# Rotation, key decay and key masks of a retention/GLA mixer on GpSimd instead of VectorE, and its constants loaded in three groups

## The reference, cut to what matters

```python
proj = rmsnorm(x, w_norm_mix) @ w_in
q_r, k_r, v_r, g_r, q_g, k_g, v_g, g_g, a_lr = split(proj)
q_r = rotary(q_r, pos)
k_r = rotary(k_r, pos) * DK ** -0.5
# retention, per chunk
scores = (q_r @ k_r.T) * decay_mask
out    = scores @ v + (q_r @ S) * q_decay
S      = S * chunk_decay + (k_r * k_decay).T @ v
# gated linear attention (GLA): the same form, with data-dependent decays exp(cumsum(log_a))
x = x + concat(norm(out_r) * silu(g_r), norm(out_g) * silu(g_g)) @ w_out
# then: rmsnorm -> PEER expert retrieval (16384 experts) -> residual -> final rmsnorm
```

## Time and profile before

| | |
|---|---|
| median of 3 runs | 4079.37 us (4070.77 to 4085.7) |
| profiled execution, its own time | 4075.24 us |
| its span, first to last instruction | 4073.5 us |
| mixer, from SyncE's first load to the first load of the next stage | 677.90 to 969.90 us, 292 us |
| TensorE matmul busy | 3608.8 us (89%) |
| VectorE busy | 2568.2 us (63%) |
| GpSimd busy | 1355.0 us (33%) |
| mean granted TensorE clock | 0.932 |

### The profile page before, as it was taken

One profiled execution on the slowest core, in us unless ns is written; L12 is line 12 of the kernel. 1 busy time (PEld: TensorE's weight loads), 2 busy tenths in 40 slices (PEclk: granted clock), 3 DMA queues, 4 the chain that ended last, 5 costly groups with the idle time before them and its releaser, 6 DMA issues. The chain is left out here.

```text
span 4073.5 us, 49975 instructions
## 1 busy us (share of the span) xinstructions
PE 3608.8 (89%) x19469; PEld 3360.9 (83%) x19469; DVE 2568.2 (63%) x3509; ACT 1083.2 (27%) x984; POOL 1355.0 (33%) x990
## 2 busy tenths in 40 slices
PE   6999996885986969987998998999599999999996
PEld 5888885664865859987998998998599999999995
DVE  4111112885213118999777777777688888898886
ACT  3222221332112213322333333332122222222222
POOL 0000000000000000111978888886154455454442
PEclk8999998776997989998999999999799999999997
DMA  4222223435323544554888989888788898989886
GB/s 161 108 108 108 108 98 109 145 120 187 132 79 140 196 156 146 218 214 172 334 332 332 345 318 354 334 318 349 289 332 334 336 353 339 357 332 357 343 328 230
DMA packets 209787, 983.08 MB, mean 241 GB/s; under 512 B 20593, under 2 KB 84401, under 8 KB 111202
## 3 DMA queue, kind: packets, MB, share of 16 engines
q1 hardware_dynamic: 130898, 523.57, 34.5%
q0 software_dynamic: 60960, 424.18, 27.2%
q10 hardware_dynamic: 17776, 33.27, 2.3%
HBM read 873.43 MB, written 107.52 MB: 241 GB/s over the span
## 5 line engine op out<-in xcount | busy, mean ns | idle before, releaser
L2062 PE MATMUL outputs_vp<-outputs_w_hi,outputs_whi 128*128 128x384 f32 x2048 | 693.0, 338 | 78.2 <-DVE outputs_w_lo L1994 41.3
L1624 PE MATMUL hidden_hp<-hidden_dense_hi,hidden_whi 128*128 128x384 f32 x2048 | 710.1, 347 | 42.0 <-DVE hidden_wlo L1408 41.9
L1625 PE MATMUL hidden_hp<-hidden_dense_lo,hidden_whi 128*128 128x384 f32 x2048 | 697.4, 341 | 0.0
L1626 PE MATMUL hidden_hp<-hidden_dense_hi,hidden_wlo 128*128 128x384 f32 x2048 | 696.5, 340 | 0.0
L2064 PE MATMUL outputs_vp<-outputs_w_hi,outputs_wlo 128*128 128x384 f32 x2048 | 691.1, 337 | 0.0
L2063 PE MATMUL outputs_vp<-outputs_w_lo,outputs_whi 128*128 128x384 f32 x2048 | 691.0, 337 | 0.0
L1553 POOL DMA_INDIRECT hidden_row<-u_rows,expert_ids x192 | 334.2, 1740 | 952.1 <-DVEq L1806 713.1
L1827 DVE CUSTOM_DVE_ANT_0 hidden_row<-hidden_row,hidden_h_row 128x2048 f32<-128x2048 f32 x192 | 439.4, 2298 | 175.2 <-DMA hidden_row<-u_rows,expert_ids 174.0
L1877 POOL DMA_INDIRECT outputs_row<-v_rows,outputs_id x192 | 321.1, 1672 | 618.9 <-DVE accg L2011 575.5
L1566 POOL TENSOR_SCALAR hidden_spare<-hidden_iota,hidden_seconds 128x128 f32<-128x128 f32 x384 | 476.1, 1252 | 122.9 <-PE hidden_tq L1609 78.2
L1404 ACT CAST outputs_whi<-outputs_raw 128x2048 fp32r<-128x2048 f32 x128 | 244.9, 1913 | 851.0 <-PE outputs_vp L2064 601.1
(11 more groups left out here) (313 smaller groups left out, 5041.4 us busy)
## 6 DMA issues: line engine op xcount, KB each, us to landing
hidden_raw<-u_units SPq DMA_DIRECT2D x128, 1024.0 KB, 8.0
outputs_raw<-v_units SPq DMA_DIRECT2D x128, 1024.0 KB, 6.5
w_in_raw<-w_in SPq DMA_DIRECT2D x48, 1024.0 KB, 5.2
hidden<-hidden_hid SPq DMA_DIRECT2D x128, 192.0 KB, 3.7
gate_mat<-hidden_big SPq DMA_DIRECT2D x12, 2048.0 KB, 14.2
outputs_w<-hidden SPq DMA_DIRECT2D x16, 1536.0 KB, 13.0
outputs_g<-gate_mat SPq DMA_DIRECT2D x16, 1536.0 KB, 21.9
w_out_raw<-w_out SPq DMA_DIRECT2D x16, 1024.0 KB, 5.7
```

Source lines behind the costliest of these rows:

```text
L1624: mm(o, un.hi[s][:, x, :], h_hi[:, x, :], start=x == 0, stop=False)
L1625: mm(o, un.hi[s][:, x, :], h_lo[:, x, :], start=False, stop=False)
L1626: ins = mm(o, un.lo[s][:, x, :], h_hi[:, x, :], start=False, stop=x == KT - 1)
L2062: mm(o, un.hi[x][:, at, :], W_hi[s][:, e, :], start=e == 0, stop=False)
```

## The change

In the mixer, `rotate` (with the decayed keys) and the making of `km` move from VectorE's program to GpSimd's, between its DMAs. `km` gets a function of its own, `mask_keys`. GpSimd's first two `move_in` come after `rotate(SMP)` and a wait for the first logarithm chain. The constants are in three groups with a semaphore each: nine for the sample tile (`const_s_in`), five for the prompt tiles (`const_in`), and `gnb` (`norm_in`). ScalarE no longer waits for constants. SyncE loads `alr` first, then `qk_r`, the nine, `qk_g`, the five, and then waits for the first rotation ahead of the samples' v and g.

```diff
+        consts_s = [(wa2, w_a2), (rope, c["rope"]), (kdec_s, c["kdec_s"]), (keep_s, c["keep_s"]), (ident, c["ident"]),
+                    (qdec_s, c["qdec_s"]), (mask_rs, c["mask_rs"]), (causal_s, c["causal_s"]), (seq_rows, c["seq_rows"])]
+        consts = [(keep, c["keep"]), (kdec, c["kdec"]), (qdec, c["qdec"]), (mask_r, c["mask_r"]), (causal, c["causal"])]
...
+            sp.wait_ge(ones_set, 1)
+            sp.dma_start(alr[0:RANK, :], alr_dram).then_inc(alr_in, 16)
             load_qk_r(SMP)
+            for tile_, src in consts_s:
+                sp.dma_start(tile_[:], src).then_inc(const_s_in, 16)
+            load_qk_g(SMP)
             for tile_, src in consts:
                 sp.dma_start(tile_[:], src).then_inc(const_in, 16)
-            sp.wait_ge(ones_set, 1)
-            sp.dma_start(alr[0:RANK, :], alr_dram).then_inc(alr_in, 16)
-            load_qk_g(SMP)
-            for n in range(3):
-                sp.dma_start(gnb[:, n, :], gn[n].partition_broadcast(P)).then_inc(const_in, 16)
+            load_qk_r(0)
             for g in range(2):
                 part(v_s[g], smp_in, SMP, (VR, VG)[g])
                 part(g_s[g], smp_in, SMP, (GR, GG)[g])
-            load_qk_r(0)
             load_vg_r(0)
             load_qk_g(0)
+            for n in range(3):
+                sp.dma_start(gnb[:, n, :], gn[n].partition_broadcast(P)).then_inc(norm_in, 16)
...
+            d = Steps(pool, pstep)
+            ptt, mult, sub = nc.gpsimd.tensor_tensor, ALU.mult, ALU.subtract
...
+            def mask_keys(k):
+                group, h = k // H, k % H
+                if group == 0:
+                    pool.wait_ge(k_decayed, 1)
+                else:
+                    pool.wait_ge(kl_copied, 1)
+                ks = (kd_s, klr_s)[group][:, h, :]
+                if k > 0:
+                    pool.wait_ge(st_made, st_at["head", k - 1, 1] + 1)
+                ptt(km[:], bcast(ks, 1, NSEQ), bcast(seq_rows[:], 2, DK), mult).then_inc(k_masked, 1)
+
+            pool.wait_ge(const_s_in, 16 * n_consts_s)
+            rotate(SMP)
+            pool.wait_ge(z_log, 1)
             move_in(0)
             move_in(1)
-            move_out(0)
-            store_r(0)
-            move_out(1)
-            for t in range(PTILES):
+            for t in [SMP] + list(range(PTILES)):
                 x, y = heads_at(t)
-                if t == 3:
+                if x is not None:
+                    if t == SMP:
+                        pool.wait_ge(const_in, 16 * n_consts)
+                    rotate((t + 1) % TILES)
+                if t != SMP:
+                    move_out(y - 2 if y else 2 * H - 1)
+                    store_r(t)
+                if x is None:
                     store_samples(1)
-                if t == 3:
                     store_g(t)
                     break
+                mask_keys(x)
                 move_out(x)
-                store_g(t)
+                if t != SMP:
+                    store_g(t)
                 if t == 1:
                     store_samples(0)
-                store_r(t + 1)
-                move_out(y)
+                mask_keys(y)
...
-            act.wait_ge(const_in, 16 * n_consts)
...
-            vec.wait_ge(const_in, 16 * n_consts)
+            vec.wait_ge(const_s_in, 16 * n_consts_s)
...
+                if t == 0:
+                    vec.wait_ge(norm_in, 48)
...
-                rotate(u)
                 mask_g_scores(t)
+                if smp:
+                    vec.wait_ge(const_in, 16 * n_consts)
...
-            pe.wait_ge(const_in, 16 * n_consts)
             pe.wait_ge(alr_in, 16)
+            pe.wait_ge(const_s_in, 16 * n_consts_s)
```

More of the change, by code:

```diff
@@ L605, in mixer @@
         s8_out = [a.gpsimd_dma_sem(f"s8_out{s}") for s in range(2)]
-        final_out, dstep, astep = a.sem("final_out"), a.sem("dstep"), a.sem("astep")
+        final_out, dstep, astep, pstep = (a.sem(s) for s in ("final_out", "dstep", "astep", "pstep"))
         block = ctx.enter_context(nc.Block())
@@ L649, in seg @@
             return at
-        n_consts = len(consts) + 3
+        n_consts_s, n_consts = len(consts_s), len(consts)
         @block.sync
@@ L737, in store_samples, with rotate @@
                                out_s[group][:].rearrange("p h v -> p (h v)")).then_inc(s_mix_stored, 16)
+            def rotate(t):
+                R, n = rows(t), front(t)
+                pool.wait_ge(qk_r_in, 16 * (n + 1))
+                cos, sin = (bcast(rope[0:R, t, x, :], 1, 8) for x in range(2))
+                x1, x2 = qk_r[0:R, :, 0:64], qk_r[0:R, :, 64:128]
+                wait(pool, r_turned, n)
+                wait(pool, k_decayed, n)
+                d(ptt(ra[0:R], x1, cos, mult))
+                d(ptt(rb[0:R], x2, sin, mult))
+                d.wait()
+                ptt(rot[0:R, :, 0:64], ra[0:R], rb[0:R], sub).then_inc(rotated, 1)
+                pool.wait_ge(rotated, 2 * n + 1)
+                d(ptt(ra[0:R], x1, sin, mult))
+                d(ptt(rb[0:R], x2, cos, mult))
+                d.wait()
+                ptt(rot[0:R, :, 64:128], ra[0:R], rb[0:R], ALU.add).then_inc(rotated, 1)
+                pool.wait_ge(rotated, 2 * n + 2)
+                if n > 1:
+                    pool.wait_ge(st_made, st_at["ret", t - 1] + 1)
+                k, by = (kd_s, kdec_s) if t == SMP else (kd, kdec)
+                ptt(k[0:R], rot[0:R, 4:8, :], bcast(by[:], 2, DK), mult).then_inc(k_decayed, 1)
@@ L879, in _ @@
             vec.wait_ge(zeros_set, 5)
-            vec.wait_ge(const_in, 16 * n_consts)
-            def rotate(t):
-                R, n = rows(t), front(t)
-                vec.wait_ge(qk_r_in, 16 * (n + 1))
-                cos, sin = (bcast(rope[0:R, t, x, :], 1, 8) for x in range(2))
-                x1, x2 = qk_r[0:R, :, 0:64], qk_r[0:R, :, 64:128]
-                wait(vec, r_turned, n)
-                wait(vec, k_decayed, n)
-                d(tt(ra[0:R], x1, cos, mult))
-                d(tt(rb[0:R], x2, sin, mult))
-                d.wait()
-                tt(rot[0:R, :, 0:64], ra[0:R], rb[0:R], sub).then_inc(rotated, 1)
-                vec.wait_ge(rotated, 2 * n + 1)
-                d(tt(ra[0:R], x1, sin, mult))
-                d(tt(rb[0:R], x2, cos, mult))
-                d.wait()
-                tt(rot[0:R, :, 64:128], ra[0:R], rb[0:R], ALU.add).then_inc(rotated, 1)
-                vec.wait_ge(rotated, 2 * n + 2)
-                if n > 1:
-                    vec.wait_ge(st_made, st_at["ret", t - 1] + 1)
-                k, by = (kd_s, kdec_s) if t == SMP else (kd, kdec)
-                tt(k[0:R], rot[0:R, 4:8, :], bcast(by[:], 2, DK), mult).then_inc(k_decayed, 1)
+            vec.wait_ge(const_s_in, 16 * n_consts_s)
             def decay_q(t):
@@ L1142, in finish_g @@
                     tt(o, o, g_g[:], mult).then_inc(g_mixed, 1)
-            rotate(SMP)
             log_decay(SMP)
```

16 lines of the change are left out of this document (3 added, 13 removed).

## The result

The changed kernel took **4089.9 us** (median of 14 runs, 4082.3 to 4095.8), the kernel before beside it 4079.6 us (14 runs): ratio **1.0023**, 95% interval 1.0013 to 1.0032. The forecast was 4075, 4.5 us faster; it became 10.3 us slower, 0.9 us above the range.

The account below looks back on a forecast made before the run. It took the mixer as bound by loads at its start, then by VectorE and TensorE handing work to and fro, VectorE waiting for scores. 8.5 - 2.5 - 1.5 = 4.5 us faster than 4079.37 gave 4075 us, range 4061 to 4089.

Parts of the forecast that it names:

- Part 5: VectorE and GpSimd meeting at SBUF, seven two-input finish_r operations held 0.27 us or less each: 1.5 us lost.
- Rival (b): VectorE held by GpSimd for whole operations in finish_r of three tiles: 2.8 us slower, 4082; chance 0.20.
- Part 3: Mixer start: gate 12 us earlier, less 1 for GpSimd's rotation and 2.5 for late g_r(0): 8.5 us gained.
- Part 1: Prompt tiles' rotation leaves VectorE, which then waits longer for TensorE's scores: 0 us.
- Part 2: Masked keys, eight operations of 1.21 us, leave VectorE and become longer waits for TensorE: 0 us.
- Part 4: Head 3's masked keys come late behind DMAs in GpSimd's queue, a new wait: 2.5 us lost.
- Rival (c): GpSimd's time follows element count, 2.43 and 4.86 us, delaying start and head 3's keys: 5.5 slower, 4085; chance 0.15.
- Rival (d): GpSimd's first operation starts late, or postponed transfers take back the gate's gain: 5 us less at start, 4080; chance 0.08.
- Rival (a): All of VectorE's relief counts: 24 us rotations, 9 key masks, 12 at the gate: 4034; chance 0.05.

Follow-up runs that it names:

- e1: The changed kernel with rotations and key masks back on VectorE, constant groups and load order kept: 4060.6 us, 0.9963 of the kernel before.
- e11: The kernel of e1 unchanged, measured once more: 4066.6 us, 0.9964 of the kernel before.
- e8: e1 plus four GpSimd memsets per pass into a buffer nobody reads: 4069.7 us, 0.9967 of the kernel before.
- e10: e1 with the samples' rotation alone on GpSimd: 4072.3 us, 0.9984 of the kernel before.
- e9: e1 with the rotations of tiles 1 to 3 on GpSimd, started only after weigh: 4068.1 us, 0.9968 of the kernel before.
- e2: The changed kernel with rotations back on VectorE and key masks still on GpSimd: 4068.4 us, 0.9985 of the kernel before.
- e4: The changed kernel with GpSimd's rotations of tiles 1 to 3 started only after weigh: 4073.2 us, 0.9996 of the kernel before.
- e12: e10 with g_r(0) loaded ahead of the samples' v and g: 4070.4 us, 0.9980 of the kernel before.

## Why the prediction was wrong

Against before, after's mixer has -8.8 at the start (`var_r(0)`), +23.7 held, -3.0 between score maskings and the next `var_r`, +0.5 at the end: +12.4. (The medians differ by 10.3; the 2 us between are within what the rest of the program scatters by: e1 and e11, one kernel, have spans 11 us apart.) By the prediction's steps:

- **Part 5, the step that failed.** "Both engines at SBUF: -1.5 us", bounds 0 and 10.2; measured 23.7 us lost in the four passes, with 24.0 held. Three errors in it. It took 0.27 us from the earlier trace rows, where GpSimd's operation is small, one-input and the one that is held; here eight large ones of GpSimd come in succession, up to three without a gap, and VectorE is the one that stands. Its upper bound priced one GpSimd operation for each of VectorE's, and a row has no such limit: 4.7 us for one operation. And it counted VectorE's seven large operations, while 16.7 of the 28.3 us held fell on nine operations of 128x4, eight of them in the variance and root chain.
- **Rival (b)**, VectorE held for whole operations, was the right mechanism, at 0.20 and 4082, and the sign named for it came: `finish_r` operations at over 2 us (5.79, twice 2.17). Its place was right only in part: `finish_r` held 7.4 us, less than the 10.2 priced there, and it left out the small operations (16.7) and the start (4.3). The Trainium skill (SBUF — State Buffer, Who interferes with whom) has the second one block fully when VectorE has two inputs in SBUF and GpSimd reads it; the traces agree for the two-input ones (5.79 for 1.22), for GpSimd's side (2.13 for 1.28) and for two-input ones beside memsets, which run at their length (0.16, e8). For one-input copies and `tensor_scalar` the same section of the Trainium skill has this only in modes that use both port pairs; L146 was held (1.12 for 0.17), and so was e8's L1085 beside a memset, but no trace shows an operation's mode. The traces go beyond the section in one way: VectorE mostly stood through several GpSimd operations. I had the rule and the row side by side and gave the row 0.52, though the row showed another pairing.
- **Part 3, 8.5 at the start: 8.0 measured**, right in sum by two errors. The gate opened 13.4 earlier (12), and the rotation on GpSimd with the late `g_r(0)` cost 5.9 in e10 (1 + 2.5). Had the rotation stayed on VectorE the gain would have been 13.4 (e1).
- **Part 1, 0**: right for the rotations of tiles 1 to 3, which e9 tries: 278.1 against 278.2.
- **Part 2, 0**: a gain was missed. e2 against e1 gives 3.6 us between score maskings and `var_r`, of 9.7 us of keys taken off VectorE.
- **Part 4, -2.5**: the wait came as forecast, TensorE 4.08 us at head 3, and cost nothing by itself in after: VectorE was held in L1125 until 807.82, past the end of TensorE's step. In e4, where less is held, VectorE waits 0.90 us there. The term was too large.
- Rival (c) is out: GpSimd took 1.26 us for 128x512 and 1.9 to 2.1 for the keys (1.3 and 2.4 forecast). Rival (d) is out as to the code load, whose 6 us (the Trainium skill, GPSIMD Engine Reference, Instruction dispatch) no trace shows between the gate and GpSimd's first operation (after issued its configuration at 678.37 and computed from 688.08, so a load that ran at once would not show); its other half, transfers put behind, is real (e12). Rival (a) is out by e9 as to the rotations; of the keys' relief 3.6 us counted.

The range missed by 0.9 us because (b) entered it at its low price. With the 24.0 us held in the four passes in place of its 10.2, its sum is 16.6 slower, 4096, an estimate from after's trace. That the measured time came within 0.9 us of the range is luck: the 3.0 us gained ahead of `var_r` and the keys of head 3, late at no cost, made up for part of the holding.

## What to carry to other kernels

Work moved from VectorE to GpSimd is not only work that takes longer there (1.26 us for 0.68, 1.91 for 1.21): while GpSimd works from SBUF, a step of VectorE's chain that runs from SBUF can stand until GpSimd's row has a gap. So before moving, ask what VectorE does in those microseconds. Beside its waits the rotations held nobody (e9, e4), and operations with an operand in PSUM ran at their length (L998). Beside the small operations behind `var_r` the samples' pass of after lost 7.5 us to a row of 12.4 (keys and rotation, 737.33 to 749.78), tile 1's 7.3 to one of 10.7. And ask what the relief is worth: here VectorE waited for TensorE right behind the rotations, and the answer was nothing for them and 3.6 us of 9.7 for the keys; the gain lay in the three groups of constants and the order of the loads, 13.6 us, and needed no GpSimd.

To read it in a profile: a held operation is *busy*, not waiting. It shows in no list of waits, only in a duration that its shape doesn't explain, and in a busy time that doesn't fall when instructions leave.

## What the runs showed that I had not expected

- VectorE is held from before GpSimd's row starts: in e2 by an operation that began at 694.37, 0.88 us ahead of the keys' row at 695.25 (0.35, 0.47 and 0.81 us in after). GpSimd was issuing DMAs just then, but the same issues held nothing in e1; beside an issue alone after has one small excess, a one-input operation at 698.98 with 0.45 for 0.28. Whether GpSimd's rows start late in the record or VectorE gives way once begun wasn't tried.
- Which side stands is not even. In after, GpSimd's operations that had waited for no semaphore took what they take alone, whatever VectorE did; those that were held in turn (2.13 for 1.28 at most) had all waited for one.
- GpSimd's one-input operation of 128x512 was slower than its product of an operand with itself, 1.47 us against 1.01, and held VectorE in shorter bits. Why wasn't tried.
